# The RWKV scan of a two-network kernel: the second direction moved to the other two corners of the array, loads no longer waited for one by one, and two evictions put in another order

## The reference, cut to what matters

```python
def step(S, inp):
    w_t, k_t, v_t, kk_t, a_t = inp[:5]
    s_kk = jnp.einsum('nbhvk,nbhk->nbhv', S, kk_t)
    S = S * w_t[..., None, :] - s_kk[..., :, None] * (kk_t * a_t)[..., None, :] + v_t[..., :, None] * k_t[..., None, :]
    y_t = jnp.einsum('nbhvk,nbhk->nbhv', S, inp[5]) if emit else None
    return S, y_t
s_final, ys = lax.scan(step, state0, seqs)
ys = jnp.moveaxis(ys, 0, 2)
y = ys[0] + jnp.flip(ys[1], axis=1)
```

## Time and profile before

| | |
|---|---|
| median of three runs | 5292.43 us |
| the profiled execution: its time, its span | 5301.3 us, 5299.5 us |
| span busy, whole program: PE, DVE, ACT, POOL | 88%, 50%, 23%, 14% |
| the scan stage | from 3290.2 us to about 3819.5 us of the span |

### The profile page before, as it was taken

The page is one execution under the profiler, slowest core; times in us unless marked ns, Lnnn a source line. Parts: engine busy times, 40 slices in busy tenths (PEclk is TensorE's granted clock), DMA queues, the critical chain, the costliest instruction groups (busy, mean ns, idle before and its releaser), DMA issues.

```text
span 5299.5 us, 72020 instructions
## 1 busy us (share of the span) xinstructions
PE 4655.1 (88%) x28852; PEld 2961.9 (56%) x28852; DVE 2666.6 (50%) x4580; ACT 1233.2 (23%) x2254; POOL 765.7 (14%) x942
## 2 busy tenths in 40 slices
PE   7987788889899989998979844899887999999998
PEld 3556634544588434554545422899644555455687
DVE  2457754621488121567476487355633444423465
ACT  2223312420011021111020264223112444301230
POOL 0014400000000000111000066665100000000000
PEclk9999999999999989999989966999998999999999
DMA  3322151112122211344112255344211111021122
GB/s 147 101 82 80 61 175 38 40 68 95 48 80 80 76 45 63 131 157 148 36 61 98 104 192 198 94 112 110 74 47 45 36 36 36 16 95 64 71 85 80
DMA packets 152501, 451.22 MB, mean 85 GB/s; under 512 B 73200, under 2 KB 73456, under 8 KB 130800
## 3 DMA queue, kind: packets, MB, share of 16 engines
q1 hardware_dynamic: 128464, 350.91, 19.5%
q0 software_dynamic: 22848, 92.29, 5.1%
q10 hardware_dynamic: 864, 3.47, 0.2%
HBM read 377.42 MB, written 69.21 MB: 84 GB/s over the span
## 4 chain that ended last, share of the span: by engine, by line
PE 60%; issue 9%; DVE 9%; POOLq 7%; PEld 5%; DMA 3%; ACT 2%; DVEq 2%; POOL 1%; PEldq 0%; SPq 0%; ACTq 0%
PE psum L386 52%; PEld psum L386 4%; POOLq L2850 3%; POOLq L2848 3%; PE psum L648 1%; PE psum L2408 1%; DVE sbuf L663 1%; PE psum L2409 1%; DVE sbuf L1113 1%; PE psum L2380 1%; DVE sbuf L2555 1%; PE psum L1051 1%; DVE sbuf L666 1%; DMA sbuf<-w_side 1%; PE psum L1266 1%
## 5 line engine op out<-in xcount | busy, mean ns | idle before, releaser
L386 PE MATMUL psum<-sbuf 128*128 128x256 f32 (+3 forms) x10160 | 3295.7, 483 | 178.2 <-DVE sbuf L1614 51.5
L386 PEld LDWEIGHTS psum<-sbuf 128*128 128x128 f32 (+1 forms) x10160 | 1917.8, 190 | 1513.0 <-issue 1178.7
L3450 PE MATMUL psum<-sbuf 64*64 64x64 f32 (+1 forms) x10752 | 425.9, 237 | 27.7 <-SPq L3359 16.2
L3450 PEld LDWEIGHTS psum<-sbuf 64*64 64x64 f32 x10752 | 411.8, 138 | 44.4 <-SPq L3359 18.3
L598 DVE CUSTOM_DVE_ANT_0 sbuf<-sbuf 128x1024 f32<-128x1024 f32 x160 | 212.4, 1327 | 39.7 <-DMA sbuf<-w_side 23.1
L1626 DVE SCALAR_TENSOR_TENSOR sbuf<-psum,sbuf 128x256 f32<-128x256 f32 (+2 forms) x288 | 125.8, 480 | 194.9 <-PE psum L386 190.4
L3575 ACT ACTIVATE sbuf<-psum 128x256 f32<-128x256 f32 (+3 forms) x384 | 128.7, 368 | 362.7 <-PE psum L3450 298.6
L3045 PE MATMUL psum<-sbuf 64*128 64x512 f32 (+2 forms) x192 | 86.9, 720 | 142.3 <-ACT sbuf L3119 64.9
L631 ACT ACTIVATE sbuf<-sbuf 128x512 f32<-128x512 f32 (+1 forms) x114 | 52.9, 551 | 620.5 <-DVEq L3749 603.3
L588 POOL DMA_DIRECT2D sbuf<-w_side x128 | 68.4, 535 | 855.5 <-DVE sbuf L598 854.8
L3045 PEld LDWEIGHTS psum<-sbuf 64*128 64x128 f32 (+1 forms) x192 | 40.0, 268 | 185.1 <-POOL sbuf L3007 69.5
(11 more groups left out here) (319 smaller groups left out, 5171.7 us busy)
## 6 DMA issues: line engine op xcount, KB each, us to landing
sbuf<-w_side POOLq DMA_DIRECT2D x128, 512.0 KB, 3.8
sbuf<-w_sgu_uz SPq DMA_DIRECT2D x32, 1088.0 KB, 5.0
sbuf<-terms SPq DMA_DIRECT2D x115, 256.0 KB, 2.8
sbuf<-w_up SPq DMA_DIRECT2D x22, 1024.0 KB, 4.8
sbuf<-w_merge SPq DMA_DIRECT2D x8, 2560.0 KB, 9.4
sbuf<-w_mla_head SPq DMA_DIRECT2D x16, 1152.0 KB, 5.1
sbuf<-w_sgu_v SPq DMA_DIRECT2D x8, 2048.0 KB, 7.7
sbuf<-w_sgu_out SPq DMA_DIRECT2D x8, 2048.0 KB, 7.8
```

What stands on the lines that cost most here:

```text
L386: last = nc.tensor.matmul(out, w, x, start=(n == 0), stop=(n == len(pairs) - 1))
L3450: last = t.matmul(out[hs], lhs[hs], rhs[hs], start=start, stop=stop)
```

## The change

The second direction (d = 1) keeps its place in SBUF for the loaded arrays, but its products are written to the other head's partitions: a matmul from rows 0 to 63 goes to columns 64 to 127 and the reverse. `heads` takes `turned` for that, and `corners` issues for each chunk the two matmuls of direction 0 and the two of direction 1 next to each other, so that four neighbours in the stream lie in the four 64x64 corners of the array. This holds for the products of part 1, for the transposes, and for the outputs (turned back). The products `w`, `corrected` and the steps' state products stay as they were, on the diagonal corners, but of data that is turned for d = 1. For this the query part of the terms and the decays are loaded a second time with the heads exchanged (`queries`, `decays_turned`), and the inverse goes to exchanged partitions.

The outputs leave the steps: all 32 of their matmuls come behind `w` (`outputs`), and the vector engine adds them behind `made` (`add_outputs`). The states of all steps are kept (`state_at`). The vector engine evicts `lbt` and `mb_b` first, then does the state of step 0, and only then the four masked products. SP issues one transfer for `terms` and two for `queries` and waits for none of them; the engines wait for the landing. `blocks(m+2)` goes behind `inverse(m)` instead of `blocks(m+1)` ahead of `terms(m, 0)`.

```diff
-        self.state = [chip.view(at + 2 * d * CH, 2, CH) for d in range(2)]
-        at += 4 * CH
...
+        at = A_W + WSLOT + D + 2 * BLK * BLK
+        self.queries = [chip.view(at + b * BATCH * CH, BATCH, CH) for b in range(BATCHES)]
+        at += BATCHES * BATCH * CH
+        self.decays_turned, at = chip.view(at, KD, NC), at + KD * NC
+        self.state = [chip.view(at + d * 2 * BATCH * CH, 2 * BATCH, CH) for d in range(2)]
+        at += 4 * BATCH * CH
+        assert at <= A_W + 2 * WSLOT, at
...
+        self.landed = [landed0, landed1, chip.sem("scan_landed2")]
...
     def y_sum(self, s, d):
 
-        return self.chip.bank(6, CH, BATCH * CH * d + CH * self.step(s, d))
+        return self.chip.bank(6 + d, CH, CH * self.step(s, d))
 
     def new(self, s, d):
 
-        return self.chip.bank(7, CH, CH * d)
+        return self.chip.bank(6, CH, BATCH * CH + CH * d)
+
+    def state_at(self, n, s, d):
+
+        i = BATCH * n + s
+        return self.state[d][:, i % (2 * BATCH)]
...
+    def landings(self, m, pos):
+        return 64 + 48 * m if pos == 0 else 48 * m + 48
...
+        def turned(m, b):
+            q = d["terms"][3 * m + b, :, 1].rearrange("p (c n e) -> p c n e", n=TERMS, e=CH)[:, :, 1]
+            for h in range(2):
+                sp.dma_start(self.queries[b][HEAD[h]], q[HEAD[1 - h]]).then_inc(self.landed[b], 16)
+
         def terms(m, b):
             sp.wait_ge(self.taken, 3 * m + b + 1)
             sp.wait_ge(b4.stored[m % 2], b4.STORED * (m // 2) + 2 * b4.STORED)
-            src = d["terms"][3 * m + b].rearrange("p d w -> p (d w)")
-            for part in range(PARTS):
-                w = slice(part * LOAD, part * LOAD + LOAD)
-                sp.dma_start(self.terms[b][:, w], src[:, w]).then_inc(self.landed, 16)
-                sp.wait_ge(self.landed, (48 * m + 16 * b - 16) * PARTS + 16 * part + 16)
-            sp.sem_inc(self.ready, 1)
+            sp.dma_start(self.terms[b], d["terms"][3 * m + b].rearrange("p d w -> p (d w)")).then_inc(self.landed[b], 16)
+            turned(m, b)
...
                 for q in range(4):
-                    to = slice(BLK * q, BLK * q + BLK)
+                    at = q ^ 2 * way
+                    to = slice(BLK * at, BLK * at + BLK)
...
+        for h in range(2):
+            sp.dma_start(self.decays_turned[HEAD[h]], b4.decays[HEAD[1 - h], :, 1]).then_inc(self.landed[0], 16)
         inverse(0)
+        turned(0, 0)
...
         for m in range(1, KD):
-            if m + 1 < KD:
-                blocks(m + 1)
             terms(m, 0)
             inverse(m)
+            if m + 2 < KD:
+                blocks(m + 2)
             terms(m, 1)
             terms(m, 2)
...
-        def heads(out, lhs, rhs, start=True, stop=True):
-            for hs in HEAD:
-                last = t.matmul(out[hs], lhs[hs], rhs[hs], start=start, stop=stop)
+        def heads(out, lhs, rhs, turned=0, start=True, stop=True):
+            for h in range(2):
+                rows = HEAD[h]
+                last = t.matmul(out[HEAD[h ^ turned]], lhs[rows], rhs[rows], start=start, stop=stop)
             return last
...
+        def corners(out, lhs, rhs, done=None):
+
+            for s in range(BATCH):
+                last = [heads(out(d)(s), lhs(d)(s), rhs(d)(s), turned=d) for d in range(2)]
+            if done is not None:
+                for d in range(2):
+                    last[d].then_inc(done[d], 1)
...
-                wait(self.ready, n)
+                wait(self.landed[pos], self.landings(m, pos))
...
+            corners(half(1, 0), term(0), term(3))
+            corners(half(1, 1), term(3), term(1), self.sums)
...
+            corners(lambda d: flat(self.slots(d, 0, 2)), term(2), pq, self.sums)
+            corners(half(2, 0), term(0), id64)
+            corners(half(2, 1), term(4), id64, self.sums)
...
-                wait(self.evacuated[d], 2 * n + 2)
-                each(at(self.half(d, 0, 0)), term(2), id64)
-                each(at(self.half(d, 0, 1)), term(3), id64).then_inc(self.token_sums[d], 1)
+                wait(self.evacuated[d], 3 * n + 2)
+            corners(half(0, 0), term(2), id64)
+            corners(half(0, 1), term(3), id64, self.token_sums)
             if past:
...
                 wait(self.tt_out[d], n + 1)
                 each(flat(self.slots(d, 1, 2)), at(inverse[1][d]), flat(self.p_lg[d])).then_inc(self.w_sums[d], 1)
+            if past:
+                outputs(*past)
...
                 heads(self.new(s, d), self.nh_h[d][:, c, 1], v[d][:, c], stop=False)
-                heads(self.new(s, d), self.a[d][:, c], self.state[d][:, s % 2], start=False).then_inc(self.state_sums[d], 1)
+                heads(self.new(s, d), self.a[d][:, c], self.state_at(n, s, d), start=False).then_inc(self.state_sums[d], 1)
+
+        def outputs(n, m, pos):
+            v = self.v[pos]
             for d in range(2):
-                c = self.step(s, d)
-                heads(self.y_sum(s, d), v[d][:, c], self.nh_h[d][:, c, 0], stop=False)
-                heads(self.y_sum(s, d), self.state[d][:, s % 2], self.qa[d][:, c], start=False).then_inc(self.y_sums[d], 1)
+                wait(self.state_ready[d], 13 * m + 4 * pos + BATCH + 1)
+            for s in range(BATCH):
+                for d in range(2):
+                    c = self.step(s, d)
+                    heads(self.y_sum(s, d), v[d][:, c], self.nh_h[d][:, c, 0], turned=d, stop=False)
+                for d in range(2):
+                    c = self.step(s, d)
+                    last = heads(self.y_sum(s, d), self.state_at(n, s, d), self.qa[d][:, c], turned=d, start=False)
+                    if s + 1 == BATCH:
+                        last.then_inc(self.y_sums[d], 1)
 
         def alone(*past):
             for s in range(BATCH):
                 step(*past, s)
+            outputs(*past)
...
             for d in range(2):
-                dve.wait_ge(self.sums[d], 3 * n + 1)
-                v.tensor_tensor(self.p_lg[d][:, :, 1], self.half(d, 1, 0), self.mask(after[d]), mult)
-                v.tensor_tensor(self.mg_g[d][:, :, 0], self.half(d, 1, 1), self.mask(before[d] + "_diag"), mult)
...
                 if past:
                     step(*past, s)
+                if s == 0:
+                    for d in range(2):
+                        v.tensor_tensor(self.p_lg[d][:, :, 1], self.half(d, 1, 0), self.mask(after[d]), mult)
+                        v.tensor_tensor(self.mg_g[d][:, :, 0], self.half(d, 1, 1), self.mask(before[d] + "_diag"), mult).then_inc(self.evacuated[d], 1)
...
-                v.tensor_tensor(self.qa[d], x[:, :, 1], c1[:, :, 0], sub)
+                if d == 1:
+                    dve.wait_ge(self.landed[pos], self.landings(m, pos))
+                v.tensor_tensor(self.qa[d], x[:, :, 1] if d == 0 else self.queries[pos], c1[:, :, 0], sub)
...
             dve.sem_inc(self.taken, 1)
+            if past:
+                add_outputs(*past)
...
-                at = m * (2 * NC) + NC * d + self.step(s, d) + self.CHUNK[pos][d]
-                v.tensor_scalar(self.state[d][:, 1 - s % 2], self.new(s, d), self.decays[:, at:at + 1], None, mult
+                at = self.step(s, d) + self.CHUNK[pos][d]
+                decay = (self.before.decays[:, m, 0] if d == 0 else self.decays_turned[:, m])[:, at:at + 1]
+                v.tensor_scalar(self.state_at(n, s + 1, d), self.new(s, d), decay, None, mult
                                 ).then_inc(self.state_ready[d], 1)
-            if s + 1 == BATCH:
-                if n == 0:
-                    dve.wait_ge(self.zeroed, 1)
-                for d in range(2):
-                    dve.wait_ge(self.y_sums[d], 4 * n + 4)
-                for d in range(2):
-                    y = self.y[:, m * NC + self.CHUNK[pos][d]:m * NC + self.CHUNK[pos][d] + BATCH]
-                    v.tensor_tensor(y, y, self.chip.bank(6, BATCH * CH, BATCH * CH * d).rearrange("p (c e) -> p c e", e=CH), add).then_inc(self.y_added[d], 1)
-                    dve.drain()
+
+        def add_outputs(n, m, pos):
+            if n == 0:
+                dve.wait_ge(self.zeroed, 1)
+            for d in range(2):
+                dve.wait_ge(self.y_sums[d], n + 1)
+            for d in range(2):
+                y = self.y[:, m * NC + self.CHUNK[pos][d]:m * NC + self.CHUNK[pos][d] + BATCH]
+                v.tensor_tensor(y, y, self.chip.bank(6 + d, BATCH * CH).rearrange("p (c e) -> p c e", e=CH), add).then_inc(self.y_added[d], 1)
+                dve.drain()
 
         def centre(m):
             y = self.row(m)
```

37 lines of the change are left out of this document (14 added, 23 removed).

## The result

The changed kernel takes 5311.51 us (median of six, 5300.44 to 5317.68), the one before 5295.12 beside it: 1.0028 of it, 95% interval 1.0017 to 1.0039. It is slower, where 5202 was forecast. The profiled execution took 5308.42 us, 7.1 more than that of before. The scan stage, by TensorE's first product in it and the first of the next stage, took 530.7 us (3293.9 to 3824.6), before 530.4 (3290.2 to 3820.6). So not one of the 90 us came. Of the 7.1, 3.7 lie ahead of the stage and 3.1 behind it, in code that is the same. Within the stage `z` of pass 3 comes 4.5 us sooner after the start (86.3 us, before 90.8), the 20 passes from there take 1.5 less, and what follows `z` of pass 23 takes 6.2 more (46.0, before 39.8). Where the rest of the 16 us between the medians lies these two executions don't tell.

What follows compares the result with a forecast made beforehand. The matrix engine was taken to bound the scan, its new chain tying with GpSimd's. `z` of pass 23 would come at 3685 instead of 3780.8, 96 us sooner, less 6: 90 off the median 5292.4 gives 5202, range 5182 to 5246.

Steps and rivals of the forecast that it cites:

- Corners halve the matmul time: Scan's cornered records: four run side by side, 14.5 and 28.5 ns instead of 29 and 57, saving 4.6 us a pass.
- The rival with serial corners: Scan's cornered records stay serial on shared rows; passes average 19.1 us, 0.9 below before; time 5263; chance 0.12.
- The new pass of 14.7 and 16.4 us: Scan pass length: 14.7 us at pos 0, 1.65 more at pos 1 and 2; a pair takes 47.4.
- steps (a) to (f): One scan pass from the end of `corrected`: 5.8 to `z`, 1.05 to `tt`, 7.65 to `corrected`, 0.2 to `made`: 14.7 us.
- I take 6 off: Scan: 6 of 96 us deducted for places where either chain is late and for `decays_turned` pieces queued before the first inverse.
- The clock, chance 0.05: Scan's granted clock falls to 1.2 GHz because busy pieces are shorter; half the passes there give 5334; chance 0.05.
- The gaps are under 2 us: Argument against the clock falling: the matrix engine's idle gaps in the new pass stay under 2 us.
- SP's 16 us of landings go: The 16.2 us waited on SP's landings of `terms` vanish, since loads are issued two passes ahead.
- The fourth rival: Scan gains nothing because loads land late, 10 us waited per pair, 70 of the 90 us lost; 5285; chance 0.03.
- the second rival: Scan's chain is 1.5 to 2 us a pass longer than counted; 35 us less gain, time 5237; chance 0.16.
- GpSimd 11 us sooner: GpSimd starts the inversion at 3316, 11 us sooner, with six small transfers (estimate 3 us) in front of `blocks(1)`.
- What follows pass 23 stays: What follows `z` of pass 23 stays as long as it was: steps lose their outputs, the outputs come behind.

Runs made afterwards that it cites:

- e4: Changed kernel plus two unwaited streams of 2016 matmul records at the scan's start, diagonal then cornered; ran once, trace only: a code piece each 3.7 us in the cornered stream.
- e8: Changed kernel with the 64 records transposing terms 2 and 3 moved from in front of step 1 to behind `tt`: 5328.82 us, 1.0038 of before.
- e19: Changed kernel loading 256 KB instead of 1280 per terms from pair 1 on, using pair 0's arrays throughout (output not the reference's): 5272.63 us, 0.9940 of before.
- e11: Changed kernel with each load of terms cut in five pieces of 256 KB, SP waiting for each: 5344.11 us, 1.0075 of before.
- e2: Kernel before with SP's part of the change alone: one unwaited transfer per terms, `blocks(m+2)` behind `inverse(m)`: 5297.24 us, 0.9989 of before.
- e3: Changed kernel without the loads of `queries`, so the second direction subtracts from the wrong head's: 5300.38 us, 0.9992 of before.
- e13: Changed kernel with queries and `decays_turned` copied by ScalarE from what is on the chip instead of loaded: 5297.32 us, 0.9984 of before.
- e9: Changed kernel with SP issuing the last store of blocks first and loading blocks for pair 1 right behind the first inverse: 5303.66 us, 0.9995 of before.
- e18: e17 without corners (all records on the diagonal) and without copies of queries: 5301.40 us, 1.0003 of before.
- e21: Kernel before with only SP's part of e17: 5283.20 us, 0.9967 of before.
- e17: Changed kernel with five-piece terms loads, SP waiting behind the second and fourth, ScalarE copying queries and decays, blocks for pair 1 first: 5277.96 us, 0.9945 of before.
- e12: Changed kernel with each load of terms in five pieces of 256 KB, SP not waiting between them: 5296.07 us, 0.9981 of before.
- e7: Changed kernel with products of direction 0 and direction 1 issued in two blocks one after the other instead of alternating: 5320.74 us, 1.0023 of before.

## Why the prediction was wrong, point by point

**Corners halve the matmul time: right.** 83 us at full clock, forecast 92. The rival with serial corners is refuted: 128 in 2.09 us in e4. So is, for this layout, the sentence of the Trainium skill ("TensorE: Matmul & The Clock Gate", Part 3, the mechanism) that a weight load overlaps matmuls in flight only when its row group differs: by it the four corners of e4, pairs of which share their rows, would have kept the 29 ns of the diagonal.

**The new pass of 14.7 and 16.4 us: 1.2 us short for the least disturbed one, 4 us short on average.** The sum of steps (a) to (f) has only signals and durations of engines in it. It lacks the term that decides: from the end of `corrected` to that of `tt` there are 336 records, 2.6 pieces of code, which it put into 6.85 us (5.8 and 1.05). By e4's 3.7 us a piece they want 9.7, 2.9 more in each pass, or 58 in 20 (an estimate); 49 us of waits on code were there. Over a whole pass of four pieces the code would want 14.8 us, as much as the forecast gave the pass, so nothing was left to catch up with. (What was expected of e8 and e19 speaks of 336 records to `z`; to `z` there are 256.) 20 passes were to take 315 us and took 398. At full clock the work was 293 us, 9 more than forecast (13.2 us a pass, and 1.5 at two of three); the clock added 40, and idleness was 66 us instead of the forecast's 31. Of the 66 only 14 were on the vector and the scalar engine, on whose signals the sum was built.

**"I take 6 off"** was the whole reserve for what the sum had left out, where all 90 were missing.

**The clock, chance 0.05: it fell,** though not as that rival had it. What went ahead of the falls is holes. All 8 holes over 2.3 us in the 20 passes were followed, within 1.4 us of their end at the latest, by 3.4 to 10.2 us at 0.50, and so were 6 of the 12 shorter ones. Shorter busy pieces alone did not do it at once: e4's bursts of 2.09 us kept 1.00 for some 50 us before it fell. "The gaps are under 2 us" was the argument against; they were up to 3.8.

**SP's 16 us of landings go: right, but they had a use.** While SP waited between pieces of 256 KB, code got through (e11). Unwaited loads bring waits on code even without corners: 22 us in e2, 4 before. The queries' transfers are not the cause, since without them (e3, e13) the holes stay. The fourth rival had loads landing late; not the loads were late, but code beside them. Its 5285 also doesn't follow from its terms: 5202 + 70 is 5272, and with the second rival's 35 it is 5307.

**GpSimd 11 us sooner: wrong,** it was 3.9, counted from the start of the stage. Beside the "six small transfers" there were four stores ahead of `blocks(1)`, which took 8.54 us behind a load of 1.3 MB, where they had taken 2.57. e9 shows that the order was at fault, by 8.8 us.

**What follows pass 23 stays: wrong by 6 us** (46.0 against 39.8), and the outputs' new place costs a fraction of a microsecond in most steps (e18 against e21). These two would have been some 13 us of correction to 5202. The step that failed is the sum (a) to (f), which put nothing for the supply of code, and with it the clock, whose fall it had at 0.05: in their place the runs show 49 us of waits on code and 40 us of slower clock in 20 passes.

## What to carry to other kernels

Before making a stream of small matmuls faster, divide its instructions (weight loads counted) by 256 and compare the time of such a piece with the 3.5 to 3.7 us at which code arrived here. Below that the stream can't be held, and faster matmuls bring only part of what the array gains: here 30 of 83 us (e17 against e18). Whether fewer and wider instructions would bring more was not tried. And a wait between transfers may be what lets code through; look at "issue" waits and at the granted clock behind them before taking it away, and try a few hundred KB in a row instead of everything or nothing.

## What the runs showed of the hardware

A matmul stream without any wait is held to one 16 KB piece of code each 3.7 us on average and 3.5 at best (e4), though the piece's own transfer takes only 1.1 us of that (81 pieces in z3 to z23 of the changed kernel, mean). Beside loads the pieces come later: none started in 6.8 us in the window above, and with a fifth of the bytes loaded the waits on code fell from 49 to 33 us (e19). That code queues behind the loads' packets on the DMA engines is the likely reason; the traces show the coincidence and the effect of fewer bytes, not the queue itself. Four 64x64 corners of fp32 run side by side at 16 ns a record with two of them on the same rows. Fourteen idle stretches of 1.4 to 1.9 us, one behind the other, passed at a clock of 1.00 before it fell; a single one of 3.78 us was followed by 0.50. That e12's five transfers in a row are better than one of the same bytes stays unexplained, and so does why e7's order of the products still overlaps.
